# The prompt's v half of a gated unit: eight block products per pair of column chunks, and seven with sums of blocks

## Chip, cores and metric

The kernel runs on one core of one Trainium2 chip. The metric is the device time of one execution, in microseconds (us). Engines are named as in the profile: PE is TensorE, DVE is VectorE, ACT is ScalarE, POOL is GpSimd, SP is SyncE, whose queue issues the weight stream.

## What is computed

One inference step of a decoder with two layers, in fp32, for 256 prompt tokens and 32 sample tokens. Layer 0 mixes tokens by latent attention, layer 1 by a gated unit; behind each come a mixture of experts and a small gated addition. The part that matters here is the v half of the gated unit in layer 1:

```python
def _sgu_project(hn, w_in, b_in, g_v, b_v):
    z = jax.nn.gelu(hn @ w_in + b_in)          # hn: tokens x 1024, w_in: 1024 x 6144
    u, v = jnp.split(z, 2, axis=-1)            # v: tokens x 3072
    return u, _layernorm(v, g_v, b_v)
...
s = einsum('grt,bntgc->bnrgc', masked w_s, v) + b_s    # mixes tokens within a chunk of 128
mix = (u * s) @ sgu_w_out                              # 3072 -> 1024
```

`hn` is the RMS-normed state. The kernel multiplies the state by the gain only, and applies a token's 1/rms behind the product.

## The kernel before

Every engine has a program of its own, written out by hand in its order; semaphores tie them. The weights come as a stream of slots of 128x2048 fp32 (1 MB), which SP loads at `load_slot` (L456) into a ring of 12 positions and some side positions. `place_slots` fixes for each slot its position and the slot held there before; SP waits until PE has freed that one (`slot_free`, to which `owe` and `free_with` add).

Layer 1's gated unit has three stages. **The v stage** (`V_UNITS`, `v_unit`): v's 3072 columns are 6 chunks of 512. A chunk's weights are two slots, each with 4 of the 8 blocks k of 128 rows. For a pair of chunks (4 slots, from `S_SGU` on) PE makes four prompt units: chunk and token block t of 128, each the sum over k = 0 to 7 of `hn_t[:, k, block t]` (stationary) by 512 columns of the slot (moving), in one PSUM bank (L2392), and then one sample unit, 32 tokens against 1024 columns in four column strips of the array at once (L2398). The first unit waits for hn's `gain` (DVE, L978) k by k. Behind the first unit come the norm sums: `tok_norm` (L2408, L2410) and `sum_norm` (L2375), for which DVE's running sum of squares L988 must be done; ACT takes the roots (L667, L921), DVE the reciprocals (L995, L1535). Then DVE takes each unit out of PSUM, `v_take` (L1525): times the token's 1/rms, plus bias. ACT applies gelu, and `v_stats` (L1532) gathers mean and variance.

**The u stage** (`z_tile`, L2422): u transposed, 24 tiles of 128 features by 288 tokens, scaled by DVE (`z_scale`, L1519). v is normalised by `tensor_scalar` (L1559) after u tile 4, and mixed over tokens from tile 7 on (`mix`, L2440; DVE's `gate_u`). **The out stage** (`out_part`, L2460) has blockwise sums of weights on DVE already (`w_sums`, L1605 to L1608). Behind it come layer 1's routing and experts, 16 pairs of experts (`gate_up`, L2278; `down`, L2287), whose weights come through the same ring.

## Time and profile before

| | |
|---|---|
| median of 3 runs | 1013.37 us (1010.97 to 1015.1) |
| the profiled execution | 1013.21 us, of which the profiled span is 1011.5 us |
| PE busy | 953.4 us, 94% of the span |
| DVE busy | 418.6 us, 41% |
| ACT busy | 179.7 us, 18% |
| v stage | 423.0 to 517.8 us |

Busy time of a PE instruction in a group overlaps its neighbours', since matmuls are pipelined; in the chain each counts only until the next starts. An fp32 matmul is two instructions in the trace (x8 in the program is x16 in a view). A busy share is an average over stages, so what a change in one stage is worth is read from that stage.

### The profile page before, as it was taken

Reading aid. Unit: us, or ns where it says so; the run is one execution under the profiler, and the core shown is the slowest. Engines: PE = TensorE matmul, PEld = TensorE weight load, DVE = VectorE, ACT = ScalarE, POOL = GpSimd, SP = SyncE. Lnnn points to the kernel's source line nnn. Section 1 sums busy time; section 2 is a strip of 40 time slices with the busy share of each in tenths; the row PEclk is TensorE's granted clock in tenths of the full one; section 3 lists DMA queues with packets and bytes.
Section 4 is the critical chain, followed back from the end, with each engine's and each line's share of the span. In section 5 each row is a group of like instructions: output and inputs, shape, how many; then the busy total and the mean of one; then the engine's idle time right before and its main releaser. Section 6 shows DMA issues by size and latency. Waiting matters only on the chain.

```text
span 1011.5 us, 14103 instructions
## 1 busy us (share of the span) xinstructions
PE 953.4 (94%) x5477; PEld 607.0 (60%) x5477; DVE 418.6 (41%) x1102; ACT 179.7 (18%) x374; POOL 69.9 (7%) x103
## 2 busy tenths in 40 slices
PE   6989999999969999999999999999999999987697
PEld 5766577555526556644468888999744444332276
DVE  3566324733320336621123878645732222121165
ACT  2123214111101113210012110001311111111123
POOL 2433000000000000000000000000111111110000
PEclk9999999999987999999999999999999999999999
DMA  9977699599999999904444324535599999999931
GB/s 355 373 225 260 259 420 371 235 421 420 421 420 412 419 422 393 422 24 167 167 182 151 103 106 132 188 126 191 201 415 418 418 417 418 418 418 423 362 137 47
DMA packets 57736, 300.29 MB, mean 297 GB/s; under 512 B 10146, under 2 KB 18530, under 8 KB 25666
## 3 DMA queue, kind: packets, MB, share of 16 engines
q1 hardware_dynamic: 47952, 282.23, 69.8%
q0 software_dynamic: 7936, 14.17, 4.2%
...
## 4 chain that ended last, share of the span: by engine, by line
PE 80%; DMA 13%; DVE 4%; issue 1%; ACT 1%; SPq 0%; DVEq 0%; POOLq 0%; ACTq 0%
PE ps L2422 9%; PE ps L2392 8%; PE ps L2278 8%; PE ps L2460 7%; PE ps L1948 6%; DMA ring_sb<-stream 6%; PE ps L2029 4%; PE ps L2287 4%; PE ps L2038 4%; PE ps L1932 3%; DMA scr_sb<-stream 3%; DMA hn_sb<-stream 3%; PE ps L1707 3%; PE ps L2071 2%; PE ps L2063 2%; PE ps L1749 2%
## 5 line engine op out<-in xcount | busy, mean ns | idle before, releaser
L2422 PE MATMUL ps<-hn_sb,ring_sb 128*128 128x288 f32 x384 | 96.3, 407 | 0.0
L2278 PE MATMUL ps<-ring_sb,scr_sb 128*64 128x512 f32 x352 | 79.8, 596 | 10.6 <-DMA ring_sb<-stream 9.8
L2392 PE MATMUL ps<-ring_sb,hn_sb 128*128 128x512 f32 x192 | 83.3, 593 | 0.0
L2422 PEld LDWEIGHTS ps<-hn_sb,ring_sb 128*128 128x128 f32 x384 | 71.6, 190 | 18.7 <-issue 0.4
L1948 PE MATMUL ps<-scr_sb,ring_sb 128*128 128x288 f32 x256 | 64.1, 406 | 0.3 <-DVE scr_sb L978 0.3
L2392 PEld LDWEIGHTS ps<-ring_sb,hn_sb 128*128 128x128 f32 x192 | 36.3, 190 | 45.0 <-issue 44.8
L2278 PEld LDWEIGHTS ps<-ring_sb,scr_sb 128*64 128x64 f32 x352 | 24.3, 137 | 63.3 <-issue 46.7
L2029 PE MATMUL ps<-scr_sb 128*128 128x128 f32 (+1 forms) x384 | 53.4, 295 | 6.1 <-issue 6.1
L1439 DVE SCALAR_TENSOR_TENSOR scr_sb<-ps,scr_sb 128x256 f32<-128x256 f32 x16 | 7.7, 484 | 122.1 <-ACT scr_sb L862 122.1
L1948 PEld LDWEIGHTS ps<-scr_sb,ring_sb 128*128 128x128 f32 x256 | 48.6, 190 | 14.1 <-DMA ring_sb<-stream 0.7
L2029 PEld LDWEIGHTS ps<-scr_sb 128*128 128x128 f32 (+1 forms) x384 | 49.7, 203 | 11.1 <-issue 7.8
L2460 PE MATMUL ps<-scr_sb,ring_sb 128*128 128x144 f32 x384 | 51.0, 286 | 0.0
L2460 PEld LDWEIGHTS ps<-scr_sb,ring_sb 128*128 128x128 f32 x384 | 48.6, 190 | 0.0
L2038 PE MATMUL ps<-ring_sb,scr_sb 128*32 128x512 f32 x384 | 45.4, 615 | 1.2 <-DMA ring_sb<-stream 1.2
L662 ACT ACTIVATE scr_sb<-h_sb 128x288 f32<-128x288 f32 x48 | 21.1, 439 | 128.4 <-DVE h_sb L1647 79.3
L540 POOL MEMSET scr_sb<- 128x1024 f32 x1 | 1.0, 951 | 616.3 <-DVE scr_sb L988 616.3
L2287 PE MATMUL ps<-ring_sb,scr_sb 128*64 128x512 f32 x176 | 41.0, 598 | 0.6 <-ACT scr_sb L866 0.5
L1525 DVE SCALAR_TENSOR_TENSOR scr_sb<-ps,scr_sb 128x512 f32<-128x512 f32 (+1 forms) x15 | 10.5, 697 | 67.3 <-PE ps L2392 60.5
L2071 PE MATMUL ps<-scr_sb 128*128 128x288 f32 x128 | 34.5, 419 | 0.0
L1707 PE MATMUL ps<-hn_sb,ring_sb 128*128 128x288 f32 x96 | 26.1, 435 | 8.8 <-DMA ring_sb<-stream 8.8
L2460 PE MATMUL ps<-scr_sb 128*128 128x144 f32 x240 | 33.5, 286 | 0.0
L1932 PE MATMUL ps<-scr_sb,ring_sb 128*128 128x288 f32 x128 | 32.1, 407 | 0.5 <-ACT scr_sb L745 0.5
...
## 6 DMA issues: line engine op xcount, KB each, us to landing
...
```

The source lines that it names most:

```text
L662: nc.scalar.activation(dst[:, k % 2, :], h_t[:, k, :], ACT.Square).then_inc(sem("h_sq"), 1)
L1707: last = mm(bank(m, T), ring(S_IN, m * D + k * P, P), hn_t[:, k, :], start=(k == 0), stop=(k == KD - 1))
L1932: last = mm(bank(m % 4, T), ring(S_O, m * D + k * P, P), oT[:, k, :], start=(k == 0), stop=(k == H - 1))
L1948: last = mm(bank(PLE_BANK[m % 4], T), ring(s, (m % 2) * D + k * P, P), HG[L][:, k, :], start=(k == 0), stop=(k == KD - 1))
L2029: last = mm(ps[:, half, k * P:(k + 1) * P], q_hn[0:tn, t, (4 * half + k) * P:(4 * half + k + 1) * P], m01[0:tn, t, :], start=(t == 0 and k ...
L2038: last = mm(ps[32 * a:32 * a + 32, 2, :], q_x[:, k, 32 * a:32 * a + 32], w[:, 512 * a:512 * a + 512], start=(k == 0), stop=(k == KD - 1))
L2071: return mm(bank(ADD_BANK[m % 3], T), q_y[:, m * P:(m + 1) * P], q_oh, start=True, stop=True)
L2278: last = mm(ps[64 * a:64 * a + 64, 2 + b, :], xT[:, k, 64 * a:64 * a + 64], slot(k // 2)[:, (k % 2) * D + a * 512:(k % 2) * D + a * 512 + ...
L2287: last = mm(ps[64 * a:64 * a + 64, 5 + n, :], aT[:, k, 64 * a:64 * a + 64], slot(4 + k)[:, a * D + n * 512:a * D + n * 512 + 512], start=( ...
L2392: last = mm(v_bank(unit), hn_t[:, k, P * t:P * t + P], ring(s, k % 4 * 512, 512), start=(k == 0), stop=(k == KD - 1))
L2422: last = mm(bank((i + 1) % 4, T), ring(s, (i % 2) * D + k * P, P), hn_t[:, k, :], start=(k == 0), stop=(k == KD - 1))
L2460: last = mm(ps[:, b, TH * n:TH * n + TH], w[:, P * i:P * i + P], x(4 * j + i), start=(start and j == 0 and i == 0), stop=(stop and j == 2 ...
```

## The change

A pair of chunks is taken as a product of blocks of two by two: tokens in two blocks of 128 (t), rows in two halves of 4 k each (h), columns in the two chunks. It is made by seven block products instead of eight, with sums of blocks ahead (of hn once for all pairs, `x_sums`; of the slots for each pair, `weight_t12`, `weight_t3`, `weight_t4`) and of products behind, all on DVE. In this text product 1 to product 7 are a pair's products in PE's order (in banks 0, 1, 2, 3, 5, 6, 7), 4 matmuls of 512 columns each. The sample unit now stands ahead of its pair's products, in bank 4. `w_t1` and `w_t2` lie in scratch; the third and fourth weight sums overwrite slots of the ring. `x_sums` takes the ring position `SPARE` for the v stage, so its slots have 11.

```diff
+V_UNITS = [u for p in range(VC // 2) for u in (("s", p, 0), ("p", 2 * p + 1, 1), ("p", 2 * p, 0), ("p", 2 * p + 1, 0), ("p", 2 * p, 1))]
...
+V_TAKEN = {u: 7 * (n // 5) + (1, 4, 5, 6, 7)[n % 5] for n, u in enumerate(V_UNITS)}
+NVP, NVT = 8 * (VC // 2), 7 * (VC // 2)
...
     for s in range(N_SLOTS):
+        if s == S_SGU:
+            spare, main = main % RING, main + 1
+            held[spare] = S_SGU + 2 * VC - 1
+        if S_SGU < s < S_SGU + 2 * VC and main % RING == spare:
+            main += 1
...
+    x_sums = ring_t[:, SPARE * SLOT:(SPARE + 1) * SLOT].rearrange("p (n k t) -> p n k t", n=4, k=4)
+    w_t1, w_t2 = scr[:, gap:gap + SLOT], scr[:, 0:SLOT]
+    v_p1, v_u2, v_u4 = tm_sr[:, 0:512], scr[:, KD * T + FF + FF // 4:KD * T + FF + FF // 4 + 512], scr[:, gap + SLOT:gap + SLOT + 512]
...
         kind, a, t = unit
-        return ps[:, (2 * a + t + 1) % 4, :] if kind == "p" else ps[:, 4 + a % 2, 0:256]
+        return ps[:, {(0, 0): 5, (1, 0): 6, (0, 1): 7, (1, 1): 3}[a % 2, t], :] if kind == "p" else ps[:, 4, 0:256]
...
             if L == 0:
                 sum_sq(nxt, KD - 1)
+                token_sums(0)
+                weight_t12(0)
                 rstd(nxt)
+        def token_sums(part):
+            a11, a12, a21, a22 = (hn_t[:, 4 * h:4 * h + 4, P * t:P * t + P] for t in range(2) for h in range(2))
+            if part == 0:
+                dve.wait_ge(sem("h_gain"), 8 * H_STAGE["mix1"] + KD)
+                link(nc.vector.tensor_tensor(x_sums[:, 0], a21, a22, ALU.add))
+                nc.vector.tensor_tensor(x_sums[:, 1], x_sums[:, 0], a11, ALU.subtract).then_inc(sem("t_sb"), 1)
+            else:
+                dve.wait_ge(sem("t_sb"), 1)
+                nc.vector.tensor_tensor(x_sums[:, 2], a11, a21, ALU.subtract)
+                nc.vector.tensor_tensor(x_sums[:, 3], a12, x_sums[:, 1], ALU.subtract).then_inc(sem("t_sb"), 1)
+        def weight_t12(p):
+            b11, b12, b21, b22 = pair_slots(p)
+            for n in (0, 2, 3):
+                dve.wait_ge(*full(S_SGU + 4 * p + n))
+            if p:
+                dve.wait_ge(sem("z_ps"), 8 * p - 4)
+            nc.vector.tensor_tensor(w_t1, b12, b11, ALU.subtract).then_inc(sem("w_sb"), 1)
+            dve.wait_ge(sem("w_sb"), 4 * p + 1)
+            nc.vector.tensor_tensor(w_t2, b22, w_t1, ALU.subtract).then_inc(sem("w_sb"), 1)
+        def weight_t3(p):
+            b11, b12, b21, b22 = pair_slots(p)
+            dve.wait_ge(sem("z_ps"), 8 * p + 1)
+            nc.vector.tensor_tensor(b12, b22, b12, ALU.subtract).then_inc(sem("w_sb"), 1)
+        def weight_t4(p):
+            b11, b12, b21, b22 = pair_slots(p)
+            dve.wait_ge(sem("z_ps"), 8 * p + 6)
+            dve.wait_ge(sem("w_sb"), 4 * p + 2)
+            nc.vector.tensor_tensor(b21, b21, w_t2, ALU.subtract).then_inc(sem("w_sb"), 1)
...
+        def v_sum_take(unit, part):
+            link(nc.vector.tensor_tensor(v_at(unit), part, v_bank(unit), ALU.add))
+            v_take(unit, v_at(unit))
...
-        for n, unit in enumerate(V_UNITS):
-            v_take(unit)
-            if n >= 2:
-                v_stats(V_UNITS[n - 2])
+        for p in range(VC // 2):
+            us, u22, u11, u12, u21 = V_UNITS[5 * p:5 * p + 5]
+            if p == 0:
+                token_sums(1)
+            weight_t3(p)
+            v_take(us, v_bank(us))
+            dve.wait_ge(sem("z_ps"), 8 * p + 2)
+            nc.vector.tensor_copy(v_p1, bank(0)).then_inc(sem("z_r"), 1)
+            if p:
+                v_stats(V_UNITS[5 * p - 2])
+            dve.wait_ge(sem("z_r"), 7 * p + 2)
+            dve.wait_ge(sem("z_ps"), 8 * p + 3)
+            link(nc.vector.tensor_tensor(v_u2, v_p1, bank(1), ALU.add))
+            if p:
+                v_stats(V_UNITS[5 * p - 1])
+            dve.wait_ge(sem("z_ps"), 8 * p + 4)
+            nc.vector.tensor_tensor(v_u4, v_u2, bank(2), ALU.add).then_inc(sem("z_r"), 1)
+            v_stats(us)
+            dve.wait_ge(sem("z_r"), 7 * p + 3)
+            dve.wait_ge(sem("z_ps"), 8 * p + 5)
+            v_sum_take(u22, v_u4)
+            nc.vector.tensor_tensor(v_u2, v_u2, bank(3), ALU.add)
+            weight_t4(p)
+            v_sum_take(u11, v_p1)
+            v_stats(u22)
+            if p + 1 < VC // 2:
+                weight_t12(p + 1)
+            dve.wait_ge(sem("z_ps"), 8 * p + 7)
+            v_sum_take(u12, v_u4)
+            v_stats(u11)
+            dve.wait_ge(sem("z_ps"), 8 * p + 8)
+            v_sum_take(u21, v_u2)
         v_stats(V_UNITS[-2])
         z_scale(0, uT[:, 0, :])
         link(v_stats(V_UNITS[-1]))
...
+        def v_sample(p):
+            wait_slots(pe, S_SGU + 4 * p, S_SGU + 4 * p + 4)
+            if p:
+                pe.wait_ge(sem("z_r"), V_TAKEN["s", p - 1, 0])
+            if p == 0:
+                pe.wait_ge(sem("pg_z"), 5)
...
+                if p == 0:
+                    pe.wait_ge(sem("h_gain"), 8 * H_STAGE["mix1"] + k + 1)
+                for j in range(4):
+                    s = S_SGU + 4 * p + 2 * (j // 2) + k // 4
+                    last = mm(ps[32 * j:32 * j + 32, 4, 0:256], hn_t[:, k, NP_:T],
+                              ring(s, k % 4 * 512 + j % 2 * 256, 256), start=(k == 0), stop=(k == KD - 1))
+                    if k == 0 and j == 0:
                         free_with(last)
-                else:
-                    for j in range(4):
-                        s = S_SGU + 2 * (2 * a + j // 2) + k // 4
-                        last = mm(ps[32 * j:32 * j + 32, 4 + a % 2, 0:256], hn_t[:, k, NP_:T],
-                                  ring(s, k % 4 * 512 + j % 2 * 256, 256), start=(k == 0), stop=(k == KD - 1))
             last.then_inc(sem("z_ps"), 1)
-            if kind == "s":
-                owe(4)
+        def v_product(b, x, w):
+            for k in range(4):
+                last = mm(bank(b), x(k), w[:, 512 * k:512 * k + 512], start=(k == 0), stop=(k == 3))
+            last.then_inc(sem("z_ps"), 1)
+        def v_prompt(p):
+            b11, b21, b12, b22 = (ring(S_SGU + 4 * p + n, 0, SLOT) for n in range(4))
+            hn = lambda h, t: (lambda k: hn_t[:, 4 * h + k, P * t:P * t + P])
+            xs = lambda n: (lambda k: x_sums[:, n, k, :])
+            if p:
+                pe.wait_ge(sem("z_r"), V_TAKEN["p", 2 * p - 2, 0])
+            v_product(0, hn(0, 0), b11)
+            pe.wait_ge(sem("t_sb"), 1)
+            pe.wait_ge(sem("w_sb"), 4 * p + 2)
+            v_product(1, xs(1), w_t2)
+            v_product(2, xs(0), w_t1)
+            pe.wait_ge(sem("t_sb"), 2)
+            pe.wait_ge(sem("w_sb"), 4 * p + 3)
+            v_product(3, xs(2), b12)
+            v_product(5, hn(1, 0), b21)
+            if p:
+                pe.wait_ge(sem("z_r"), V_TAKEN["p", 2 * p - 1, 0])
+            v_product(6, xs(3), b22)
+            if p:
+                pe.wait_ge(sem("z_r"), V_TAKEN["p", 2 * p - 2, 1])
+            pe.wait_ge(sem("w_sb"), 4 * p + 4)
+            v_product(7, hn(1, 1), b21)
+            owe(4)
...
-        for unit in V_UNITS:
-            v_unit(unit)
-            if unit == V_UNITS[0]:
+        for p in range(VC // 2):
+            v_sample(p)
+            if p == 0:
                 tok_norm()
                 sum_norm("mix1")
+            v_prompt(p)
```

The other edits renumber waits: ACT's gelu waits for `V_TAKEN[unit]`, the u stage counts from `NVP` and `NVT` (PE's u tiles 0 to 3 wait for z_r 19, the second prompt take of the last pair), `t_sb` by 2 and `w_sb` by 12 more in the out stage.

What stands on PE around the start of the v stage, before (L1948 is the last product of the part ahead, L2392 the prompt's units, L2398 the sample's, the others the norm sums):

```order
L1948 MATMUL ps<-scr_sb,ring_sb 128x288 x48
L2392 MATMUL ps<-ring_sb,hn_sb 128x512 x8
L2408 MATMUL ps<-const_sb,scr_sb 128x1 x2
L2410 MATMUL ps<-const_sb,scr_sb 32x1 x4
L2375 MATMUL ps<-scr_sb,const_sb 128x288
L2392 MATMUL ps<-ring_sb,hn_sb 128x512 x24
L2398 MATMUL ps<-ring_sb,hn_sb 32x256 x32
L2392 MATMUL ps<-ring_sb,hn_sb 128x512 x32
```

And in the change (L2475 is the sample's unit, L2516 to L2458 the norm sums, L2484 the block products; those with scr_sb read weight sums in scratch, those with ring_sb alone read `x_sums` and a slot):

```order
L2031 MATMUL ps<-scr_sb,ring_sb 128x288 x48
L2475 MATMUL ps<-ring_sb,hn_sb 32x256 x32
L2516 MATMUL ps<-const_sb,scr_sb 128x1 x2
L2518 MATMUL ps<-const_sb,scr_sb 32x1 x4
L2458 MATMUL ps<-scr_sb,const_sb 128x288
L2484 MATMUL ps<-ring_sb,hn_sb 128x512 x4
L2484 MATMUL ps<-scr_sb,ring_sb 128x512 x8
L2484 MATMUL ps<-ring_sb 128x512 x4
L2484 MATMUL ps<-ring_sb,hn_sb 128x512 x4
L2484 MATMUL ps<-ring_sb 128x512 x4
L2484 MATMUL ps<-ring_sb,hn_sb 128x512 x4
L2475 MATMUL ps<-ring_sb,hn_sb 32x256 x32
```

The sample's unit moved ahead of the norm sums, and four matmuls on plain blocks stand between these and the first products on sums.

DVE at the same place, before, from the addition for the last k (L974), its gain (L978) and the sum of squares (L988) to the first takes of units:

```order
L974 TENSOR_TENSOR h_sb<-h_sb,scr_sb 128x288
L978 TENSOR_SCALAR hn_sb<-h_sb,par_sb 128x288
L988 TENSOR_TENSOR scr_sb<-scr_sb 128x288
L995 RECIPROCAL std_rstd_sb<-std_rstd_sb 128x288
L1535 RECIPROCAL scr_sb<-scr_sb 128x3
L1525 SCALAR_TENSOR_TENSOR scr_sb<-ps,scr_sb 128x512 x3
```

And in the change, from the same gain on (L1533 to L1538 are `token_sums`, L1547 and L1549 `weight_t12`, L1555 `weight_t3`, L1576 the scaling of a take):

```order
L988 TENSOR_SCALAR hn_sb<-h_sb,par_sb 128x288
L998 TENSOR_TENSOR scr_sb<-scr_sb 128x288
L1533 TENSOR_TENSOR ring_sb<-hn_sb 128x512
L1534 TENSOR_TENSOR ring_sb<-ring_sb,hn_sb 128x512
L1547 TENSOR_TENSOR scr_sb<-ring_sb 128x2048
L1549 TENSOR_TENSOR scr_sb<-ring_sb,scr_sb 128x2048
L1005 RECIPROCAL std_rstd_sb<-std_rstd_sb 128x288
L1590 RECIPROCAL scr_sb<-scr_sb 128x3
L1537 TENSOR_TENSOR ring_sb<-hn_sb 128x512
L1538 TENSOR_TENSOR ring_sb<-hn_sb,ring_sb 128x512
L1555 TENSOR_TENSOR ring_sb<-ring_sb 128x2048
L1576 SCALAR_TENSOR_TENSOR scr_sb<-ps,scr_sb 128x256
```

Four sums stand ahead of the reciprocals, and three behind them, before the first take.

DVE behind product 4 of the first pair (L1580 and L1576 are a take, L1613 a partial sum, L1562 `weight_t4`, L1587 statistics, L1547 and L1549 the next pair's `weight_t12`):

```order
L1580 TENSOR_TENSOR scr_sb<-scr_sb,ps 128x512
L1576 SCALAR_TENSOR_TENSOR scr_sb<-scr_sb 128x512
L1613 TENSOR_TENSOR scr_sb<-scr_sb,ps 128x512
L1562 TENSOR_TENSOR ring_sb<-ring_sb,scr_sb 128x2048
L1580 TENSOR_TENSOR scr_sb<-scr_sb,ps 128x512
L1576 SCALAR_TENSOR_TENSOR scr_sb<-scr_sb 128x512
L1587 BN_STATS scr_sb<-scr_sb 128x6
L1547 TENSOR_TENSOR scr_sb<-ring_sb 128x2048
L1549 TENSOR_TENSOR scr_sb<-ring_sb,scr_sb 128x2048
L1580 TENSOR_TENSOR scr_sb<-scr_sb,ps 128x512
L1576 SCALAR_TENSOR_TENSOR scr_sb<-scr_sb 128x512
```

Between two takes of prompt units there was one statistics row before; now the fourth weight sum stands ahead of the second take, and the next pair's two sums ahead of the third.

## Rows read from the trace of the kernel before

**Rows 1.** the page: busy time and share of the span of each engine, instructions
```profile
PE 953.4 (94%) x5477; PEld 607.0 (60%) x5477; DVE 418.6 (41%) x1102; ACT 179.7 (18%) x374; POOL 69.9 (7%) x103
```

**Rows 2.** chain that ended last, 423 to 518 us: start, length, what
```profile
423.02 6.87 PE ps L2392 x16
...
431.08 20.60 PE ps L2392 x48
451.68 3.59 PE ps L2398 x64
455.27 27.66 PE ps L2392 x64
...
517.78 0.44 PE ps L2422
```

**Rows 3.** VectorE's groups by shape, 423 to 560 us
```profile
L1525 DVE SCALAR_TENSOR_TENSOR scr_sb<-ps,scr_sb 128x512 f32<-128x512 f32 x12 | 9.0, 750 | 60.5 <-PE ps L2392 60.5
L1532 DVE BATCH_NORM_STATS2 scr_sb<-scr_sb 128x6 f32<-128x512 f32 x12 | 8.1, 682 | 0.0
...
L1559 DVE TENSOR_SCALAR scr_sb<-scr_sb 128x3072 f32<-128x3072 f32 x2 | 3.8, 1876 | 0.0
L995 DVE RECIPROCAL std_rstd_sb<-std_rstd_sb 128x288 f32<-128x288 f32 x1 | 2.0, 1952 | 4.9 <-ACT std_rstd_sb L667 4.9
```

**Rows 4.** the same view over the whole span
```profile
L1415 DVE COPY scr_sb<-ps 128x512 f32<-128x512 f32 x16 | 10.9, 681 | 0.0
...
L1605 DVE TENSOR_TENSOR scr_sb<-ring_sb 128x512 f32<-128x512 f32 x12 | 8.2, 686 | 4.5 <-PE ps L1909 3.2 <-PE ps L2460 1.3
...
L1005 DVE TENSOR_TENSOR scr_sb<-scr_sb 128x1152 f32<-128x1152 f32 x1 | 1.4, 1359 | 0.3 <-ACT scr_sb L648 0.3
```

**Rows 5.** timeline of VectorE, 422 to 427 us
```profile
422.54 0.37 DVE L978 TENSOR_SCALAR hn_sb<-h_sb,par_sb 128x288 f32<-128x288 f32 x1
...
425.84 0.37 DVE L978 TENSOR_SCALAR hn_sb<-h_sb,par_sb 128x288 f32<-128x288 f32 x1
426.31 0.46 DVE L988 TENSOR_TENSOR scr_sb<-scr_sb 128x288 f32<-128x288 f32 x1
```

**Rows 6.** L456, SyncE's slot loads, issues from 396.2 to 396.9 us
```profile
L456 SPq DMA_DIRECT2D ring_sb<-stream x2: 485/538/591, 396.2 to 396.9; - x2
...
DMA to landing us min/median/max: 14.6/15.6/16.5
```

**Rows 7.** stretches: length, busy us of engines, granted clock, DMA share, GB/s
```profile
423.00:518.00 95.00, 95.00 (x400) 43.26 (x399) 21.58 (x35) 12.83 (x21) 0.00 (x0) 1.00 0.31 125
735.00:850.00 115.00, 115.00 (x623) 50.94 (x621) 27.96 (x70) 19.19 (x36) 19.09 (x19) 1.00 1.02 418
300.00:304.00 4.00, 0.00 (x0) 0.00 (x0) 0.00 (x0) 0.00 (x0) 0.00 (x0) 0.51 1.01 412
304.00:310.00 6.00, 5.88 (x24) 5.43 (x25) 0.00 (x0) 0.60 (x1) 0.00 (x0) 0.50 1.02 423
382.00:384.00 2.00, 1.75 (x12) 0.44 (x16) 0.03 (x1) 0.50 (x2) 0.00 (x0) 0.50 1.02 422
```

**Rows 8.** waits of SyncE's queue, 517 to 850 us: total, times, longest
```profile
SPq L456 <- PE ps L2460: 64.6, 9, 8.1
SPq L456 <- PE ps L2278: 52.6, 32, 5.2
```

**Rows 9.** timeline of VectorE, 620 to 622 us
```profile
620.05 0.46 DVE L1577 TENSOR_TENSOR scr_sb<-scr_sb 128x288 f32<-128x288 f32 x1
620.43 0.68 DVE L1605 TENSOR_TENSOR scr_sb<-ring_sb 128x512 f32<-128x512 f32 x1
621.14 0.69 DVE L1606 TENSOR_TENSOR scr_sb<-scr_sb,ring_sb 128x512 f32<-128x512 f32 x1
621.75 0.68 DVE L1607 TENSOR_TENSOR ring_sb<-ring_sb 128x512 f32<-128x512 f32 x1
```

**Rows 10.** chain that ended last, 824 to 1012 us
```profile
866.47 31.80 DMA ring_sb<-stream
```

More of the change, by code:

```diff
@@ L71 @@
 VC = 6
-V_UNITS = [u for p in range(VC // 2) for u in (("p", 2 * p, 0), ("p", 2 * p, 1), ("p", 2 * p + 1, 0), ("p", 2 * p + 1, 1), ("s", p, 0))]
+V_UNITS = [u for p in range(VC // 2) for u in (("s", p, 0), ("p", 2 * p + 1, 1), ("p", 2 * p, 0), ("p", 2 * p + 1, 0), ("p", 2 * p, 1))]
 V_AT = {u: n + 1 for n, u in enumerate(V_UNITS)}
-NV = len(V_UNITS)
+V_TAKEN = {u: 7 * (n // 5) + (1, 4, 5, 6, 7)[n % 5] for n, u in enumerate(V_UNITS)}
+NVP, NVT = 8 * (VC // 2), 7 * (VC // 2)
 H_STAGE = {"ffn0": 0, "ple0": 1, "mix1": 2, "ffn1": 3, "ple1": 4, "fin": 5}
@@ L109, in place_slots @@
             side[S_PROJ[1] + n] = RING + SIDE_AT.index(n % 18)
-    table, held, uses, main = [], {}, {}, 0
+    table, held, uses, main, spare = [], {}, {}, 0, None
     for s in range(N_SLOTS):
+        if s == S_SGU:
[3 more added lines that the diff above has]
+            main += 1
         if s in side:
@@ L117, in place_slots @@
         table.append((pos, uses[pos], held.get(pos)))
-        held[pos] = s
-    return table
-SLOT_AT = place_slots()
+        held[pos] = max(s, held.get(pos, 0))
+    return table, spare
+SLOT_AT, SPARE = place_slots()
 USES0 = [sum(pos == SIDE0 + n for pos, _, _ in SLOT_AT) for n in range(2)]
@@ L340, in program @@
     b_bc = scr[:, KD * T:KD * T + FF + FF // 4]
+    x_sums = ring_t[:, SPARE * SLOT:(SPARE + 1) * SLOT].rearrange("p (n k t) -> p n k t", n=4, k=4)
+    w_t1, w_t2 = scr[:, gap:gap + SLOT], scr[:, 0:SLOT]
+    v_p1, v_u2, v_u4 = tm_sr[:, 0:512], scr[:, KD * T + FF + FF // 4:KD * T + FF + FF // 4 + 512], scr[:, gap + SLOT:gap + SLOT + 512]
+    assert KD * T + FF + FF // 4 + 512 <= FT * T and gap + SLOT + 512 <= SCR - 2 * SLOT - 256
     vsT = bs.rearrange("p g r -> p (g r)")[:, 512:512 + FT * NS_].rearrange("p (f t) -> p f t", f=FT)
@@ L1509, in ple_part, with pair_slots @@
                 sum_sq(nxt, KD - 1)
+                token_sums(0)
+                weight_t12(0)
                 rstd(nxt)
+        def pair_slots(p):
+            return [ring(S_SGU + 4 * p + n, 0, SLOT) for n in (0, 2, 1, 3)]
+        def token_sums(part):
[26 more added lines that the diff above has]
+            nc.vector.tensor_tensor(b21, b21, w_t2, ALU.subtract).then_inc(sem("w_sb"), 1)
         experts0()
@@ L2417, in z_tile @@
             if i >= 4:
-                pe.wait_ge(sem("z_r"), NV + i - 3)
+                pe.wait_ge(sem("z_r"), NVT + i - 3)
             else:
-                pe.wait_ge(sem("z_r"), NV - 1)
+                pe.wait_ge(sem("z_r"), NVT - 2)
             for k in range(KD):
@@ L2483, in out_part @@
                 if i == 0:
-                    pe.wait_ge(sem("t_sb"), (2, 3, 4)[j])
+                    pe.wait_ge(sem("t_sb"), (4, 5, 6)[j])
                 products(1, 0, j, a11, u(0, 0), True, False)
                 products(1, 1, j, a12, u(1, 0), False, False)
-                pe.wait_ge(sem("w_sb"), g + 1)
+                pe.wait_ge(sem("w_sb"), 2 * VC + g + 1)
                 last = products(1, 2, j, s2, lambda k: t2[:, k, :], False, True)
```

32 lines of the change are left out of this document (9 added, 23 removed).

## The prediction

> **What bounds the kernel now.** I read the page first, for which engine is full, then the chain of work that ended last over the stage that changes, then the timeline at the stage's start, then VectorE by groups, and last the DMA queue and the stages behind. TensorE is busy for 94% of the span [rows 1]. In the v stage, from 423 to 518 us, the chain is nothing but TensorE: the prompt's matmuls of L2392 follow one another and the sample's of L2398 without a piece in between that waits [rows 2]. In it the clock is granted in full, VectorE is busy for 21.58 us of 95, DMA for 31% [rows 7], and VectorE's takes of L1525 wait 60.5 us for TensorE [rows 3]. So a matmul less in this stage is time less at its end, if whatever feeds the others keeps up.
>
> **What is removed.** Each 128x512 product in fp32 is two instructions in the trace. The piece of 64 takes 27.66 us, the one of 48 takes 20.60, the first 16 take 6.87 [rows 2], and the piece of 64 comes twice: 82.79 us for 192, 0.431 us each. (The mean of 592 ns in a table overlaps its neighbour; the pitch is what counts.) The change has 7 x 4 products per pair in place of 8 x 4, so 168 instructions in place of 192: 24 x 0.431 = **10.35 us less**. The sample's 3.59 us per pair [rows 2] only move to the pair's start.
>
> **What is added on VectorE.** The trace of before has no 128x2048 sum, so I bound it. Two-input fp32 sums took 0.686 us for 512 columns and 1.359 for 1152 [rows 4]: 1.05 ns a column, so 2048 columns are 0.686 + 1536 x 1.05 ns = 2.30 us. That is the upper end. The lower is the rate of the one-input L1559, 1.876 us for 3072 columns [rows 3], 0.61 ns each: 1.25 us. I take 2.30, since the nearest rows are the same operation on the same kinds of tile. The Trainium skill (VectorE: DVE Perf Modes, "The perf-mode tier table") says that two-input fp32 operations have no doubled mode while one-input ones have, and gives 2293 ns for 2048 columns; by that the upper value holds and the sum is the one below, by the lower one the stall below would be gone and the time 1002.9. Sums of 512 follow each other at 0.61 us, or 0.71 where the second waits for the first [rows 9]. A take is now a sum out of PSUM and a scaling, 0.75 + 0.75 by L1525 [rows 3], and the copy of the first product is 0.68 by L1415 [rows 4].
>
> Per pair that makes four sums of 2048 (9.2 us), four takes of 1.5 (6.0), copy and three partial sums (0.68 + 3 x 0.75 = 2.9), the sample's take 0.5, and statistics of 4 x 0.68 + 0.4 (3.1): 21.7 us, against a pair of 3.59 + 28 x 2 x 0.431 = 27.7 us on TensorE. VectorE has room, so only the order matters.
>
> **First pair: the one wait that is not covered.** Before, the first product of each k started as soon as its gain was there. After, the sample comes first. Gain 7 ends at 425.84 + 0.37 = 426.21 and gain 6 at 422.91 [rows 5]; the sample's pass, 0.45 us a k from 423.02, reaches k = 7 at 426.2 and ends at 426.7. The norm matmuls wait for the sum of squares L988, which ends at 426.77 [rows 5], and they with L2375 take 1.20 us (from 423.02 + 6.87 = 429.89 to 431.08 [rows 2]), so to 428.0. Product 1 needs only slots and hn: 3.45 us, to 431.5. Product 2 needs x_sums 0 and 1 and both weight sums. VectorE starts these behind L988, at 426.7 (a next one starts 0.4 after the start of such a sum, as L1605 does behind L1577 [rows 9]): 0.71 + 0.61 to 428.04, 2.32 to 430.36, 2.30 to 432.66, and 0.04 until TensorE sees it: 432.70. TensorE stands for 1.2 us. Without any wait product 2 would begin at 423.02 + 3.59 + 1.20 + 3.45 = 431.26, so this start costs **1.44 us**. The slots are no part of it: the fourth issue, at 396.9, landed after 16.5 us, at 413.4 [rows 6], and that one slot of the ring is now held for x_sums only moves each of the first four to a position that is as long free; the slot that goes without a free one is the twelfth, which comes when pair 0 is done, some 25 us before it is read.
>
> **Further waits, all covered.** (a) Product 4 needs x_sums 2, 3 and the third weight sum, which overwrites a slot once the sample is done. VectorE: 432.66, reciprocal 1.95 [rows 3], the token reciprocal and its link 0.2, two sums 1.3, 2.30: 438.4. TensorE gets there at 432.70 + 6.90 = 439.6. Cover 1.2 us. (b) Product 7 needs the fourth weight sum, issued when product 5 ends; product 6 lies between, 3.45 against 2.30 + 0.1. Cover 1.0 us, three times, if VectorE is through with the take of product 4 and its sum, 3 x 0.75 = 2.3 of the 3.45 of product 5: it is. (c) The next pair's two sums: after product 5's end come 2.4, take 1.6, statistics 0.7, then 4.6, in all 9.3; TensorE asks for them 6.9 + 3.59 + 3.45 = 13.9 after it. (d) Banks: product 1 of the next pair needs the second prompt take, 4.0 after product 5's end, against 6.9 + 3.59. (e) The end: the first u tile asks for the last pair's second prompt take, 4.0 against 6.9; the last statistics come behind the first u tile's scaling as before, so the normalisation, on which the mixing waits, keeps its distance from the u tiles. Products 2 and 3 of the last pair read the region that later holds u, and are long done.
>
> **The sum.** 10.35 - 1.44 = 8.9 us. The profiled execution took 1013.21 us with a span of 1011.5; the three runs have a median of 1013.37, so it stands for them. 1013.2 - 8.9 = **1004.3 us**. Nothing behind the stage is tied to the clock on the wall: SP's stream waits there for TensorE's L2460 and L2278 [rows 8], and even where the transfers are the chain (31.8 us of it from 866 on [rows 10], DMA at 1.02 of its share from 735 to 850 [rows 7]) they began when TensorE freed their slots, so they shift with it.
>
> **Rivals.**
> 1. The forecast, 8.9 us less: chance 0.80, own range 1002 to 1007.
> 2. The second expert stage gives it back. It is full of transfers, and its end hangs on them. If the stream's start did not move, all of the gain would be lost: about 1013. For it: the full DMA [rows 7]. Against it: the queue was idle or waiting for TensorE before that stage [rows 8]. A half loss is 1008.5. Chance 0.07.
> 3. The clock. Around the idle stretch from 300 to 304 us the grant was at half, 0.51, and still 0.50 from 304 to 310 with TensorE busy [rows 7]; that gap was 4 us long. A short one, from 382 to 384, shows 0.50 too, with TensorE busy for 1.75 of 2 us [rows 7], so the new gap of 1.2 us is not safe by its shortness; but it stands behind 40 us of full work. If it cost as much as that row's six busy microseconds at half, 3 us would be lost: 1007.3. The Trainium skill (TensorE: Matmul & The Clock Gate, "Why this matters for your kernels") warns of idle gaps between bursts of matmuls for this reason; the trace agrees at 300 us. Chance 0.06.
> 4. The other side: the big sums on VectorE are much slower than their columns say, because all four read ring slots and two write into one. With d for their time, the waits are: start 1.44 + 2(d - 2.3); (a) 3d + 431.6 against 2d + 435.0, so d - 3.4; (b) 3(d - 3.35); (c) 2 x (3d + 2.2 - 13.9 - (d - 3.35)). They eat the whole gain at d = 4.4 and at d = 5 make 6.8 + 1.6 + 5.0 + 3.3 = 16.7 us, so 1013.2 + 6.3 = 1019.5. Against it: in-place sums on a ring slot, L1607, run at the pitch of the others [rows 9], and L988 took the same 0.46 at 426 us [rows 5] as L1577 at 620 [rows 9]. Chance 0.03.
> 5. The products of four steps don't keep the pitch of 0.431, because each closes a bank and opens another: 21 openings of some 0.2 us, a weight load laid bare, would be 4 us, 1008.5. The u stage opens banks as often without it. Chance 0.04.
>
> A measurement of this kernel tells about 0.5%, 5.1 us, from no change. Faster than 1008.3: case 1, case 3 and half of 5: 0.88. Within: case 2 and the rest of 5: 0.09. Slower than 1018.4: case 4, 0.03. The range of 1001.5 to 1008 takes in the bound of 1.25 us a sum (1002.9), the clock case, d up to 3.6 (start 4.0, (a) 0.2, (b) 0.8, so 5.0 in place of 1.44: 1007.9), and the spread of 4 us of the three runs.
>
> **What would show it.** Of the chain from 423 us: sample first, product 1, then one wait of 1.2 us for VectorE's second 2048 sum, and none before products 4 and 7; the stage from 423 to the first u tile 86 us in place of 94.8; the big sums at 2.3 us; VectorE busy some 70 of 86 us (3 x 21.7, and the four token sums and two reciprocals); the second expert stage moved by 9 us as a block with the same waits for transfers. Wrong would be: waits of TensorE on w_sb in pairs 1 and 2, a pitch above 0.431, the clock under 1.00 behind the gap, or a first expert transfer that starts no earlier.

## The result, and the profile after

| | before | changed |
|---|---|---|
| median of 11 runs each, in turns | 1014.76 us (1010.97 to 1016.82) | 1008.54 us (1004.03 to 1011.37) |
| the profiled execution | 1013.21 us, span 1011.5 | 1010.3 us, span 1008.6 |
| v stage in the profile | 94.76 us | 86.35 us |

The ratio is 0.9943, with a 95% interval of 0.9927 to 0.9959: 5.8 us less (4.2 to 7.4), where 8.9 had been forecast. The page of the changed kernel, first line, against [rows 1]:

```profile
PE 945.2 (94%) x5453; PEld 604.0 (60%) x5453; DVE 463.2 (46%) x1142; ACT 179.8 (18%) x374; POOL 69.9 (7%) x103
```

TensorE has 24 instructions fewer and VectorE is busy 45 us longer. The chain that ended last, 415 to 530 us (start, length, what), against [rows 2]:

```profile
424.27 0.02 issue
...
429.38 2.30 DVE scr_sb L1547
431.68 0.02 issue
431.70 2.30 DVE scr_sb L1549
434.00 0.14 issue
434.14 20.84 PE ps L2484 x48
454.98 3.59 PE ps L2475 x64
458.57 24.23 PE ps L2484 x56
482.80 3.59 PE ps L2475 x64
486.39 24.23 PE ps L2484 x56
510.62 7.76 PE ps L2530 x32
```

The stage runs from 424.27 to 510.62 us. From 434.14 on it is TensorE alone again, in pieces of 48 and 56 where there were 48 and 64. Ahead of that, two sums of VectorE are in the chain. VectorE's timeline there (start, length, instruction), and TensorE's for the same place:

```profile
427.55 0.46 DVE L998 TENSOR_TENSOR scr_sb<-scr_sb 128x288 f32<-128x288 f32 x1
428.05 0.69 DVE L1533 TENSOR_TENSOR ring_sb<-hn_sb 128x512 f32<-128x512 f32 x1
428.77 0.69 DVE L1534 TENSOR_TENSOR ring_sb<-ring_sb,hn_sb 128x512 f32<-128x512 f32 x1
429.38 2.28 DVE L1547 TENSOR_TENSOR scr_sb<-ring_sb 128x2048 f32<-128x2048 f32 x1
431.70 2.29 DVE L1549 TENSOR_TENSOR scr_sb<-ring_sb,scr_sb 128x2048 f32<-128x2048 f32 x1
```

```profile
429.37 3.59 PE L2484 MATMUL ps<-ring_sb,hn_sb 128*128 128x512 f32 x8
434.14 7.10 PE L2484 MATMUL ps<-scr_sb,ring_sb 128*128 128x512 f32 x16 [1.18 <-DVE scr_sb L1549]
441.08 3.60 PE L2484 MATMUL ps<-ring_sb 128*128 128x512 f32 x8
```

The bracket is the new gap: 1.18 us for the second weight sum. The waits of TensorE from 423 to 511 us (total, times, longest) hold no other, and the clock is granted in full over the same stretch (second view, columns as in [rows 7]; the 1.00 behind the engines):

```profile
PE ps L2484 <- DVE scr_sb L1549: 1.2, 1, 1.2
```

```profile
423.00:511.00 88.00, 86.73 (x383) 39.73 (x382) 66.92 (x78) 12.62 (x21) 0.00 (x0) 1.00 0.32 130
```

So the stage gave 94.76 - 86.35 = 8.41 us. What it gave did not arrive whole. The tail is the last gated addition behind the experts. There TensorE first transposes the sums of the experts' rows (`combine`, L2449 and L2451), and a filler matmul L1779 (`fill`) stands ahead of them. From the first transpose to `turn_out`, which stands directly behind its last product, it took 40.7 us before, 44.7 after. TensorE's timeline at its start, changed kernel:

```profile
945.14 3.65 PE L2370 MATMUL ps<-ring_sb,scr_sb 128*64 128x512 f32 x16 [0.47 <-ACT scr_sb L876]
949.95 0.70 PE L1779 MATMUL ps<-const_sb 128*128 128x256 f32 x2 [1.16 <-issue]
952.99 0.71 PE L2449 MATMUL ps<-const_sb,scr_sb 128*128 128x128 f32 x3 [2.34 <-DVE scr_sb L1758]
953.63 1.33 PE L2451 MATMUL ps<-scr_sb 128*128 128x288 f32 x2
```

The same place in the kernel before:

```profile
953.10 3.65 PE L2287 MATMUL ps<-ring_sb,scr_sb 128*64 128x512 f32 x16 [0.47 <-ACT scr_sb L866]
958.01 0.70 PE L1696 MATMUL ps<-const_sb 128*128 128x256 f32 x2 [1.26 <-issue]
959.98 0.58 PE L2366 MATMUL ps<-const_sb,scr_sb 128*128 128x128 f32 x3 [1.27 <-DVE scr_sb L1675]
960.50 0.75 PE L2368 MATMUL ps<-scr_sb 128*128 128x288 f32 x2
```

The wait ahead of the transposes is 2.34 us in place of 1.27, and the products behind it take 1.33 us in place of 0.75. Stretches of the changed kernel (columns as in [rows 7]) say why the products take longer: the clock is granted at 1.2 GHz in place of 2.4 (0.50 at half; 0.53 where a piece at full clock is in the stretch).

```profile
950.00:953.00 3.00, 0.66 (x3) 0.26 (x3) 1.89 (x3) 1.42 (x2) 0.00 (x0) 1.00 1.08 322
953.00:964.00 11.00, 11.00 (x30) 6.90 (x31) 6.21 (x15) 1.77 (x4) 0.00 (x0) 0.53 0.85 347
964.00:975.00 11.00, 11.00 (x49) 8.24 (x48) 4.96 (x13) 2.11 (x5) 0.00 (x0) 1.00 0.00 1
```

Before, every stretch there had 1.00, also the thin one ahead of the transposes and the one with them:

```profile
955.00:960.00 5.00, 2.47 (x13) 0.64 (x9) 2.64 (x4) 2.17 (x3) 0.00 (x0) 1.00 1.07 307
960.00:965.00 5.00, 4.71 (x21) 3.00 (x22) 2.98 (x6) 0.44 (x1) 0.00 (x0) 1.00 1.00 401
```

### The profile page after: what moved, and what is told of

Same layout as the page of the kernel before. It is cut to its first block, busy times and chain, and to the rows that moved or that the text cites. A ratio compares the mean times of both kernels' runs of the same rounds, so it can differ in the third digit from the quotient of the medians.

```text
span 1008.6 us, 14123 instructions
## 1 busy us (share of the span) xinstructions
PE 945.2 (94%) x5453; PEld 604.0 (60%) x5453; DVE 463.2 (46%) x1142; ACT 179.8 (18%) x374; POOL 69.9 (7%) x103
## 4 chain that ended last, share of the span: by engine, by line
PE 77%; DMA 15%; DVE 5%; issue 1%; ACT 1%; SPq 0%; DVEq 0%; POOLq 0%; ACTq 0%
PE ps L2530 9%; DMA ring_sb<-stream 8%; PE ps L2361 8%; PE ps L2569 8%; PE ps L2484 7%; PE ps L2031 6%; PE ps L2370 4%; PE ps L2112 3%; PE ps L2015 3%; DMA scr_sb<-stream 3%; PE ps L2154 3%; PE ps L2121 3%; DMA hn_sb<-stream 3%; PE ps L1790 2%; PE ps L2146 2%; PE ps L1832 2%
## 5 line engine op out<-in xcount | busy, mean ns | idle before, releaser
L2361 PE MATMUL ps<-ring_sb,scr_sb 128*64 128x512 f32 x352 | 79.8, 596 | 10.0 <-DMA ring_sb<-stream 9.3
L2361 PEld LDWEIGHTS ps<-ring_sb,scr_sb 128*64 128x64 f32 x352 | 24.3, 137 | 62.4 <-issue 44.2
L2569 PE MATMUL ps<-scr_sb,ring_sb 128*128 128x144 f32 x384 | 51.0, 286 | 0.0
L2569 PEld LDWEIGHTS ps<-scr_sb,ring_sb 128*128 128x128 f32 x384 | 48.6, 190 | 0.0
L2569 PE MATMUL ps<-scr_sb 128*128 128x144 f32 x240 | 33.5, 286 | 0.0
L1454 DVE TENSOR_SCALAR scr_sb<-ps,scr_sb 128x512 f32<-128x512 f32 x16 | 12.0, 751 | 45.6 <-PE ps L2370 45.6
L2484 PE MATMUL ps<-ring_sb,hn_sb 128*128 128x512 f32 x72 | 32.6, 595 | 0.0
L2361 PE MATMUL ps<-scr_sb 128*64 128x512 f32 x120 | 27.6, 597 | 4.4 <-DMA scr_sb<-stream 4.4
```

Source lines behind the costliest of these rows:

```text
L2361: last = mm(ps[64 * a:64 * a + 64, 2 + b, :], xT[:, k, 64 * a:64 * a + 64], slot(k // 2)[:, (k % 2) * D + a * 512:(k % 2) * D + a * 512 + ...
L2484: last = mm(bank(b), x(k), w[:, 512 * k:512 * k + 512], start=(k == 0), stop=(k == 3))
L2569: last = mm(ps[:, b, TH * n:TH * n + TH], w[:, P * i:P * i + P], x(4 * j + i), start=(start and j == 0 and i == 0), stop=(stop and j == 2 ...
```

## The experiments

Theory: the stage behaves as forecast, and some 3 us of its gain are given back in the tail, where TensorE's clock falls behind a longer wait. Rivals: the new gap of 1.2 us costs clock time (the prediction's third case), the other order of units has an effect of its own, the comparison came out small by chance.

Three lengths are read in each profile: "stage" is from the start of the v stage to the first u tile, "tail" from the first transpose to `turn_out`, and "rest" from the start of the v stage to the end of the span, which leaves out the part ahead, where the code is the same and which took from 421.3 to 425.3 us in the profiles (it has stretches at half clock of its own, 10 to 24 us in all). "gap" is the wait just ahead of the first transpose, "half" the time at 1.2 GHz at the tail. Ratios are medians against the kernel before, run in turns on the same chip.

| kernel | ratio (95%) | stage | tail | rest | gap | half |
|---|---|---|---|---|---|---|
| before (first profile) | 1 | 94.8 | 40.7 | 588.6 | 1.27 | 0 |
| changed (first profile) | 0.9943 (0.9927 to 0.9959) | 86.3 | 44.7 | 584.4 | 2.34 | 10.2 |
| e5, before again | 0.9985 (0.9965 to 1.0005) | 94.9 | 40.4 | 588.2 | 1.18 | 0 |
| e1, changed again | 0.991 (0.988 to 0.994) | 86.3 | 41.7 | 581.1 | 1.96 | 3.4 |
| e4, changed, tail filled | 0.9888 (0.9862 to 0.9913) | 86.3 | 40.1 | 579.7 | filled | 0 |
| e14, e4 once more | 0.9912 (0.9889 to 0.9934) | 86.3 | 40.1 | 579.6 | filled | 0 |
| e6, before, tail filled | 0.9992 (0.9977 to 1.0007) | 94.9 | 40.2 | 588.4 | filled | 0 |
| e11, before without filler | 1.0016 (1.0002 to 1.003) | 94.8 | 44.3 | 592.4 | 3.45 | 10.2 |
| e13, before, rows later | 1.003 (1.0014 to 1.0047) | 94.8 | 43.2 | 592.1 | 2.14 | 6.8 |
| e2, new gap filled | 0.9934 (0.9912 to 0.9956) | 86.3 | 43.2 | 582.8 | 1.89 | 6.8 |
| e8, new gap longer | 1.0005 (0.9992 to 1.0019) | 92.6 | 44.3 | 589.6 | 1.93 | 10.2 |
| e3, product 5 second | 0.9904 (0.9881 to 0.9926) | 84.9 | 44.4 | 582.0 | 1.60 | 10.2 |
| e10, e3 and e4 | 0.9893 (0.9873 to 0.9913) | 84.9 | 40.3 | 577.9 | filled | 0 |
| e9, an eighth product | 1.0017 (0.9999 to 1.0036) | 96.6 | 40.2 | 591.3 | 1.13 | see e9 |
| e7, before, sample first | 0.9991 (0.9974 to 1.0009) | 95.2 | 40.6 | 588.7 | 1.29 | 0 |
| e12, count padded | 0.9926 (0.9905 to 0.9946) | 86.3 | 43.2 | 582.4 | 1.53 | 6.8 |

### e1 and e5: both kernels once more

No edit.

> The changed kernel again. In the profile of the changed kernel the v stage was 8.4 us shorter (forecast 8.9) and the shift was still 7.4 us at the second expert stage, but only 2.9 us at the end, with the clock at half from about 953 to 964 us. Theory A: where half-clock stretches fall differs from execution to execution, and only such stretches stand between 8.4 us and the measured difference; then this run lies 6 to 9 us under the kernel before in executions of equal mean clock, and its profile may have the shift whole at the end. Theory B: the change itself brings the clock down, by the new gap or by narrow matmuls at the v stage's start; then the mean clock is lower here than in the kernel before by 0.002 or more in most executions, and profiles show half clock behind 430 us.

> The kernel before, submitted as an experiment, so that each execution lists its mean clock. Theory A: ratio 1.000 within 0.002, mean clocks spread like those of the changed kernel (0.981 to 0.991), time falling by about 0.35 to 0.5 us for each us of half clock less. Theory B: mean clock higher than the changed kernel's by 0.002 to 0.004.

The stage came out at 86.3 and 94.9 us again, and the clock fell at the tail in the changed kernel alone, this time for 3.4 us, so the tail cost 1.3 us more than before's. e5 is the same program as the kernel before and its median came out 1.9 us under it (the interval takes in 1), so a difference of 1 or 2 us between medians of one comparison is read from the profiles' stretches, not from the medians. The mean granted clock of whole executions does not tell the kernels apart (0.9855 in e1's six, 0.9865 in e5's twelve, 0.9849 in the 23 of the kernel before beside them), since the stretches at half in the part ahead outweigh the tail's. How long the tail's fall lasts varies from one execution to the next; it was there in all six profiles of kernels with the changed stage, seven products and no filler added at the tail (the first, e1, e2, e3, e8, e12), for 3.4 to 10.2 us.

### e4, e14 and e6: the tail's wait filled

Five more filler matmuls behind the one that is there, so within TensorE's wait for the sums of the experts' rows, in the changed kernel (e4, and e14 once more) and in the kernel before (e6):

```diff
             pe.wait_ge(sem(f"y_sb{L}"), 2 * PAIRS)
+            for _ in range(5):
+                fill(7)
```

> The changed kernel with five more filler matmuls of 256 columns (2.2 us in all) on TensorE while it waits for the rows of experts to come back, before the last gated addition. Theory A with the tail as its main place: the half-clock stretch of 953 to 964 us goes or comes seldom, mean clock up by 0.002 or more, 2 to 4 us faster than the changed kernel. If the lottery is elsewhere: same time as the changed kernel within 1 us, since the filler lies in idle time.

> The changed kernel with filler matmuls in the tail's gap, once more, beside the kernel above. If the tail's clock is what the change lost: 10 to 11 us faster than the kernel before (ratio 0.988 to 0.991), no half clock behind the experts' last product. If that first result came by chance: 0.993 to 0.995 as the changed kernel itself.

> The kernel before with the same five filler matmuls ahead of the last gated addition. If the tail's clock fall is common to both kernels: faster than before by the same 2 to 4 us as the filler gives the changed kernel. If only the changed kernel has it there: no change from before, 0.998 to 1.002.

TensorE's timeline in e4, and a stretch of its granted clock:

```profile
950.24 2.86 PE L1779 MATMUL ps<-const_sb 128*128 128x256 f32 x12 [1.15 <-issue]
952.93 0.56 PE L2451 MATMUL ps<-const_sb,scr_sb 128*128 128x128 f32 x3
953.42 0.75 PE L2453 MATMUL ps<-scr_sb 128*128 128x288 f32 x2
```

```profile
950.00:964.00 14.00, 13.76 (x63) 10.11 (x63) 10.68 (x24) 4.15 (x8) 0.00 (x0) 1.00 0.88 335
```

The transposes start no earlier and run at full clock. The tail is 40.1 us. e4's median is 1003.77 us beside e1's 1007.3 on the same chip, 3.5 us less, but with six runs each they overlap (the means lie 2.2 apart). e14's ratio falls nearer to the first expectation (0.988 to 0.991) than to the second, though its interval touches 0.993. Taken together it is clearer: the 29 runs of the first comparison, e1, e2 and e12 have a mean of 0.9929 of the kernel before's median on their chip, the 12 runs of e4 and e14 0.9900, which is 2.9 us less (1.7 to 4.1). The same filler gives the kernel before nothing measurable (2.3 us at most by e6's interval), and neither of its two profiles, nor e7's, has the fall. So the loss is in the tail, it is the clock's, and the kernel before has it seldom, if at all.

### e13 and e11: the kernel before with a longer wait at that place

e13 holds VectorE up ahead of the sums of rows by two copies in place; e11 leaves out the filler that the kernel before has:

```diff
             dve.wait_ge(sem(f"y12_in{half}"), 48)
+            if half == 0:
+                for _ in range(2):
+                    link(nc.vector.tensor_copy(y12[:, 1, 0, 0:512], y12[:, 1, 0, 0:512]))
```

```diff
             pe.wait_ge(sem("e_oh"), QUADS + 1)
-            fill(7)
```

> The kernel before, with one thing added: ahead of the first sums of the experts' rows, VectorE makes two copies in place of 512 columns each, linked to these sums, so that the sums, and with them TensorE's transposes, start some 0.8 us later. The gap of TensorE ahead of the transposes should grow from some 1.2 us to about 2.0 us. If a gap of this length is enough for the granted clock to fall (my theory of the tail): half clock for some us between 955 and 970 us in the profile, 42 to 44 us from the first transpose to turn_out's where the kernel before has 40.4 us, and 1.5 to 4 us slower in all, of which 0.8 us at most is the delay itself. If it takes a gap as long as the 3.45 us of the kernel without its filler (rival), or something else of the changed kernel than the gap: the clock stays at 1.00, 40.4 us, and at most 0.8 us slower.

> The kernel before without the one filler matmul (0.7 us) that it has in its tail, so that TensorE stands for about 3.2 us ahead of the transposes in place of 1.3 and 1.3. If the length of that gap decides whether the clock falls (theory: the changed kernel's second gap of 1.9 to 2.3 us, against 1.2 in the kernel before, is what costs it its clock), half clock in the profile at 950 to 970 us, the part from first transpose to turn_out 43 us or more in place of 40.4, and 2 to 4 us slower than before. If the fall has another cause in the changed kernel: no change.

TensorE at the tail of e13, and its clock:

```profile
962.48 0.58 PE L2369 MATMUL ps<-const_sb,scr_sb 128*128 128x128 f32 x3 [2.14 <-DVE scr_sb L1678]
...
964.11 1.33 PE L2371 MATMUL ps<-scr_sb 128*128 128x288 f32 x2
```

```profile
965.00:970.00 5.00, 5.00 (x13) 2.95 (x12) 3.66 (x11) 1.44 (x4) 0.00 (x0) 0.50 1.00 416
```

And e11's:

```profile
959.00:971.00 12.00, 11.03 (x31) 6.90 (x32) 7.42 (x18) 2.12 (x6) 0.00 (x0) 0.57 0.83 334
```

With nothing of the change in it, the kernel before loses its clock too when this wait is 2.14 us in place of some 1.25: half for 6.8 us, a tail of 43.2 us, and 1.4 to 4.8 us slower, of which 0.9 is the delay itself (the first transpose stands 538.0 us behind the v stage's start, before 537.1). The rival in the expectation, that it takes a wait as long as e11's 3.45 us or something else of the change, is out: a longer wait at this place is enough. Where the fall begins is not the same, though: in e13 the clock fell 1.5 us behind the start of the first transposes, in e11 0.8 us ahead of it. e11 lost 0.2 to 3.0 us by its median, 3.8 in its one profile.

### e2 and e8: the new gap filled, and made longer

e2 puts three fillers between product 1 and product 2 of the first pair. e8 makes the first weight sum three times for pair 0, so TensorE waits some 4.6 us longer:

```diff
             v_product(0, hn(0, 0), b11)
+            if p == 0:
+                for _ in range(3):
+                    fill(5)
```

```diff
+            if p == 0:
+                for _ in range(2):
+                    link(nc.vector.tensor_tensor(w_t1, b12, b11, ALU.subtract))
             nc.vector.tensor_tensor(w_t1, b12, b11, ALU.subtract).then_inc(sem("w_sb"), 1)
```

> The changed kernel with three filler matmuls of 256 columns (1.3 us) in the new gap of the first pair, between product 1 and product 2. Theory A (the gap costs only its 1.2 us): same time as the changed kernel within 0.5 us, stage length the same within 0.2 us. Theory B (the gap brings the clock down in part of the executions): 1 to 3 us faster than the changed kernel, mean clock higher.

> The changed kernel with the first weight sum of pair 0 made three times, which makes the new gap 4.6 us longer (5.8 us). By the sum of waits alone: 4.6 us slower than the changed kernel, and the third weight sum another 3.4 us late against a cover of about 1, with 4.6 us of it bought by the gap, so nothing more. With a clock that falls after such a gap: 3 us or more on top, half clock in the profile from about 437 us.

e2 has the changed kernel's stage, 86.3 us, a ratio within its interval, and its fall at the tail: the new gap of 1.2 us costs itself and nothing of the clock. In e8 the gap is 5.82 us and the clock falls behind it:

```profile
437.96 7.48 PE L2487 MATMUL ps<-scr_sb,ring_sb 128*128 128x512 f32 x13 [5.82 <-DVE scr_sb L1552]
```

```profile
433.00:436.00 3.00, 0.00 (x0) 0.00 (x0) 2.93 (x3) 0.00 (x0) 0.00 (x0) 0.75 0.00 0
436.00:442.00 6.00, 4.04 (x6) 1.85 (x7) 5.93 (x6) 0.00 (x0) 0.00 (x0) 0.56 0.00 0
```

The stage grew by 6.3 us for 4.6 us of waiting; the median is 6.6 us above e2's on the same chip. So the prediction's third case has its mechanism at this place with a gap of 5.8 us, and did not come with one of 1.2.

### e3 and e10: product 5 ahead of product 2

Product 5 (bank 5, plain blocks) stands directly behind product 1, so TensorE has work while VectorE sums; VectorE's waits are renumbered, and the fourth weight sum moves behind the sum `v_u4`. e10 has e4's filler too.

```diff
             v_product(0, hn(0, 0), b11)
+            v_product(5, hn(1, 0), b21)
...
             v_product(3, xs(2), b12)
-            v_product(5, hn(1, 0), b21)
```

> The changed kernel with product 5, which needs no sum, moved behind product 1 in every pair, and the fourth weight sum made as soon as it is done. It covers the new gap with 3.45 us of work. By my sum: the wait of 1.2 us goes, no other comes, stage 85.1 us in place of 86.3, so 1.2 us faster than the changed kernel; Theory B adds another 1 to 3 us.

> The changed kernel with product 5 behind product 1 and the five filler matmuls in the tail. The reordering gave a stage shorter by 1.4 us (84.9 against 86.3), the tail filler 3.5 us by the median against the changed kernel, and the two places are 430 us apart: if they add, 1002 to 1003 us where the kernel before has 1014, ratio 0.987, part from first transpose to last stage 40.2 us in the profile and no half clock from 945 to 965 us. If the filler's gain was chance: as the reordered kernel alone, ratio 0.990.

The stage is 84.9 us in both, 1.4 less than with the gap: product 2 follows at 434.90 without a wait. By medians e3 lies below e2 on the same chip, 0.9904 against 0.9934, which is 3 us where the gap explains 1.4, but the intervals overlap; and e10 (0.9893) lies no lower than e4 and e14. The 0.987 that e10's expectation added up was not reached. In the rest e10 has the least of all, 577.9 us against 588.4 of e6. The intervals of e4, e10 and e3 lie below that of the changed kernel's first comparison; their medians don't tell which is the best.

e3's tail shows something that the table hides. Its clock was at half before the transposes began (stretches ahead of them, columns as in [rows 7], then the first transposes, 0.93 us in place of 0.58):

```profile
947.90:948.80 0.90, 0.07 (x1) 0.00 (x0) 0.90 (x3) 0.88 (x2) 0.00 (x0) 1.00 1.11 255
948.80:949.50 0.70, 0.00 (x0) 0.00 (x0) 0.41 (x1) 0.00 (x0) 0.00 (x0) 0.51 1.02 246
```

```profile
949.56 0.93 PE L2449 MATMUL ps<-const_sb,scr_sb 128*128 128x128 f32 x3 [1.60 <-DVE scr_sb L1758]
```

The filler had ended at 947.97, so TensorE had waited 0.85 us when the clock fell, less than the whole wait of the kernel before. In e8 it was 0.8 us. In the first profile of the change, e1, e2 and e12 the clock fell 0.3 to 0.9 us behind the start of the transposes.

### e9: an eighth product in each pair

Product 6 is made twice, all else as changed:

```diff
+            for k in range(4):
+                mm(bank(6), xs(3)(k), b22[:, 512 * k:512 * k + 512], start=(k == 0), stop=(k == 3))
             v_product(6, xs(3), b22)
```

> The changed kernel with product 6 of each pair computed twice (the first time its result is overwritten), so with eight products of work and all the sums. The products' part by itself: 10.35 us more than the changed kernel, so 1.2 to 2 us above the kernel before: what the sums, the gap and the new order cost without the saving. If the loss against the forecast comes with the change's own structure and not from chance, this stands 4 to 5 us above the kernel before.

The stage is 10.3 us longer than the changed kernel's, 24 x 0.431 = 10.35 by the prediction's term, and the gain is gone: 1.7 us above the kernel before (-0.1 to 3.7), as the expectation's first case has it. Here the fall came elsewhere: 1.00 up to 954 us, then this, and 1.00 again, during the experts' last product, which took 5.35 us in place of 3.65:

```profile
954.00:958.00 4.00, 3.94 (x12) 1.21 (x14) 0.00 (x0) 0.01 (x1) 0.00 (x0) 0.57 1.04 315
```

Ahead of it TensorE had waited 1.36, 1.22 and 0.47 us between pieces of work. So the last wait alone does not say when the clock falls. All the falls lie in the stretch with little work from 940 us on, which the kernel before has too (TensorE busy for 3.09, 3.30 and 2.47 us of each 5 from 945 to 960 us).

### e7 and e12: order alone, and the number of instructions

e7 is the kernel before with its sample unit first in each pair (one line of `V_UNITS`, with the waits moved along). e12 is the changed kernel with 12 one-column matmuls in the new gap, which brings TensorE's count back to 5477:

```diff
+                for _ in range(12):
+                    mm(ps[0:32, 5, 0:1], q_sq[:, NP_:T], ones[:, 0:1], start=True, stop=True)
```

> The kernel before with the sample unit ahead of its pair's prompt units, nothing else: the order of the change without its products and sums. No wait on sums exists, so the stage should stay at 94.8 us, at most 0.1 more for the sample's wait on the last gain; ratio 0.999 to 1.001. Its instruction count on TensorE is that of the kernel before: if the tail's pattern hangs on the stage's order, the gap ahead of the transposes is 1.9 us or more here too; if it hangs on the stream of instructions, it is 1.2.

> The changed kernel with twelve matmuls of one column in the new gap of the first pair, which take no time there (0.5 us in an idle 1.2) and bring TensorE's count of instructions back to that of the kernel before. In the five profiles with the smaller count the last pair of experts shows waits of about 0.5, 1.8, 0.8 us and then 1.6 to 2.3 us ahead of the transposes; in the four with the old count 1.4, 0.3, 0.6, 1.4 and then 1.1 to 1.3. If the count (where code is fetched) makes the difference: the old pattern here, the tail's clock full, 2 to 3 us faster than the changed kernel. If the shift in time makes it: the changed kernel's pattern and time.

The order alone does nothing that can be measured (0.9991), though its stage is 0.3 us longer where 0.1 at most was expected. e12 was made for a difference at the last pair of experts: TensorE's waits for its weights are 1.41, 0.28 and 0.56 us before, 0.46, 1.83 and 0.83 in the changed kernel. Padding brought the pattern of before back (1.25, 0.28, 0.57), yet the gap ahead of the transposes was 1.53 us, the clock fell for 6.8 us, and the time is the changed kernel's. That pattern is not the cause of the fall.

## Why the prediction was right and where it was wrong

**The saving.** 24 x 0.431 = 10.35 us: right. The pitch is 24.23 / 56 = 0.433. The 160 instructions from product 2 on take 69.30 us, 0.34 more than 160 x 0.431, so the fifth case (a slower pitch) did not come in the size of 4 us that it had. e9 gives 10.3 us back for the same 24.

**The sums on VectorE.** 2.30 us was taken of a range from 1.25: measured 2.28 and 2.29 for 2048 columns. The fourth case is out. By the Trainium skill (VectorE: DVE Perf Modes, "The perf-mode tier table") two-input fp32 sums have no faster mode; the trace agrees.

**The start.** Forecast 1.44 us lost, with a wait of 1.2. The wait was 1.18. From 424.27 us to product 2 at 434.14 took 9.87 us, against 3.59 + 1.20 + 3.45 = 8.24 without a loss, so 1.63. With 0.34 of pitch that is 10.35 - 1.63 - 0.34 = 8.38 us; the stage shows 8.41.

**The covered waits.** None before products 4 and 7 or between pairs, as said. VectorE was busy for 66.9 of 88 us around the stage, some 70 of 86 forecast.

**The second expert stage.** It moved as a block: first `gate_up` 733.6 to 726.2 us, last one 950.4 to 942.4, which is 8.7 and 9.3 us less when counted from each v stage's start. SP's waits there are as [rows 8] (64.5 for the out stage's L2569, 53.7 for L2361 up to 842 us). The second case is out.

**The step that failed** is the last sentence of the sum, that nothing behind the stage is tied to the clock on the wall and all shifts with it. The starts did shift; the durations behind 950 us did not stay. What comes in its place: the experts' rows go out to memory and back before the last transposes. The last write (POOL), the read (SP) and VectorE's first sum, changed kernel:

```profile
933.92 0.96 POOL L577 DMA_INDIRECT y_rows<-scr_sb  x1 [15.56 <-DVE scr_sb L1454]
942.77 3.19 SPq L517 DMA_DIRECT2D scr_sb<-y_rows  x6
950.70 1.89 DVE L1758 TENSOR_TENSOR scr_sb<-scr_sb 128x512 f32<-128x512 f32 x3 [1.03 <-DMA scr_sb<-y_rows]
```

And before:

```profile
941.34 0.96 POOL L567 DMA_INDIRECT y_rows<-scr_sb  x1 [15.20 <-DVE scr_sb L1444]
949.54 2.98 SPq L507 DMA_DIRECT2D scr_sb<-y_rows  x6
957.95 1.89 DVE L1675 TENSOR_TENSOR scr_sb<-scr_sb 128x512 f32<-128x512 f32 x3 [0.33 <-DMA scr_sb<-y_rows]
```

From the write's issue to the sum is 16.8 and 16.6 us, and 16.3 in the mean of the six profiles, 16.4 in that of the three of the kernel before, again, and in another order (e7): the round trip is the same. From the same write to the start of TensorE's last product for the experts is 11.22 us (945.14) and 11.76 (953.10), 11.1 in the mean of the six (10.45 to 11.43) and 11.5 of the three (11.40 to 11.76). TensorE is earlier there against the rows, so its wait for their sums is longer: 1.53 to 2.34 us in the six, 1.18 to 1.29 in the three. e13 and e4 show the rest: with a longer wait the clock falls in the kernel before too, and with filler in it it does not in the changed one. The fall cost 1.3 to 4.3 us in the six profiles against a tail of 40.4, 3.2 in the mean. 8.4 - 3.2 = 5.2 us, and 5.8 was measured.

Of the 4.2 us by which 1008.54 lies above the forecast of 1004.3, some 1.5 are none of the change's: the forecast starts from 1013.2, and the kernel before took 1014.76 in the comparison.

The third case had the mechanism and the size, 3 us, but put it behind the new gap, which e2 shows to be harmless, and gave it 0.06. Looking only at the gap that the change makes was the error: the waits that were there already, next to such a fall, should have been looked through as well. The trace of before had the place: the tail's filler with waits of 1.26 and 1.27 us around it, in the stretch from 955 to 960 us, where TensorE is busy for 2.47 of 5 us.

**What stays open.** Why TensorE reaches its last product some 0.5 us earlier against the rows in the changed kernel: e12 rules the number of instructions out as the cause of the fall, and the waits for the last weights differ, but no run set them apart. And what decides the moment of the fall: in e3 and e8 it came 0.8 us into the wait, after a filler with 1.12 us of idle time ahead of it, and up to that moment TensorE had stood no longer than in the kernel before, which kept its clock; in e9 it came ahead of the wait. So that a longer wait there can cost the clock is shown (e13, e11); that its length is what cost it in each of the six profiles is not.
